# A two-block layer kernel on Trainium2: order of small matmuls among array tiles, order of DMA requests, place of a mean, and the form of eight units of products

## What is computed

```python
for i in range(2):                                   # first block
    u = rmsnorm(h) @ w_in[i]                         # 2048 -> 5632
    a_val, a_glu, a_z, q, k, v, b_z = split(u)
    ya = silu(layernorm(conv31(a_val * sigmoid(a_glu)))) * silu(a_z)
    yb = banded_attention(q, k, v, bias, sink) * silu(b_z)   # 16 heads of 64
    h = h + concat(ya, yb) @ w_out[i]
    h = h + rmsnorm(p[i] @ w_pe[i]) * sigmoid(h @ w_pg[i])
# second block: h @ w_in_2 -> RWKV-7 scan (16 heads of 64) and latent attention (8 heads),
# @ w_out_2, then a gated FFN of width 5632 with a convolution of width 3, and a last norm
```

## Time and profile before

| | us |
|---|---|
| median of 3 runs | 2280.56 |
| lowest, highest | 2279.8, 2282.35 |
| the profiled execution, whole | 2274.88 |
| its span in the trace | 2273.1 |
| PE busy in it | 2222.8 (98%) |
| PEld, DVE, ACT, POOL busy | 1968.8, 1690.8, 1068.1, 553.8 |
| DMA | 384.93 MB, 169 GB/s |
| request of a unit (1 MB) to landing, median | 4.8 |
| POOL's split of a unit (L241), mean | 4.6 |

### The profile page before, as it was taken

How to read it: one execution, slowest core, us unless ns; L and a number is a source line. 1 busy time by engine, 2 the same in 40 slices (tenths; PEclk the granted TensorE clock), 3 DMA queues, 4 the chain that set the end, 5 groups by cost and what they waited for, 6 DMA issues and landing times.

```text
span 2273.1 us, 39333 instructions
## 1 busy us (share of the span) xinstructions
PE 2222.8 (98%) x14865; PEld 1968.8 (87%) x14865; DVE 1690.8 (74%) x2863; ACT 1068.1 (47%) x1427; POOL 553.8 (24%) x226
## 2 busy tenths in 40 slices
PE   7999999999999999999999999999999999999997
PEld 6888998888888988899999887888888888888886
DVE  7688668885888488888878655778888885447887
ACT  5444464444444554556545522444444443334444
POOL 4776631017667520210002302110000000000012
PEclk9999999999999999999999999999999999999999
DMA  7445345555545355554444300455555555555564
GB/s 256 158 179 178 140 167 186 185 185 186 181 164 179 131 184 185 185 200 165 153 165 174 93 2 20 148 185 185 185 185 189 189 191 187 185 185 187 187 218 166
DMA packets 69034, 384.93 MB, mean 169 GB/s; under 512 B 15088, under 2 KB 22768, under 8 KB 23984
## 3 DMA queue, kind: packets, MB, share of 16 engines
q1 hardware_dynamic: 68912, 383.22, 47.6%
HBM read 380.02 MB, written 3.18 MB: 169 GB/s over the span
## 4 chain that ended last, share of the span: by engine, by line
PE 85%; DVE 5%; issue 3%; POOL 2%; ACT 2%; DMA 2%; SPq 0%; POOLq 0%; DVEq 0%; ACTq 0%
PE ps L259 40%; PE ps L260 21%; PE ps L247 4%; PE ps L249 4%; PE ps L248 4%; PE ps L262 3%; DMA raw<-weights_dram 1%; PE ps L870 1%; POOL low L241 1%; POOL ssq L1130 1%; DVE low L234 1%; PE ps L851 1%; PE ps L1939 1%; DVE ps L709 1%; PE ps L859 1%
## 5 line engine op out<-in xcount | busy, mean ns | idle before, releaser
L259 PE MATMUL ps<-opA,whi 128*128 128x512 f32 x2340 | 828.4, 394 | 1.5 <-POOL low L241 1.5
L229 ACT ACTIVATE whi<-raw 128x2048 fp32r<-128x2048 f32 x346 | 660.2, 1909 | 87.3 <-DMA raw<-weights_dram 85.6
L260 PE MATMUL ps<-opA,low 128*128 128x256 f32 x2496 | 672.6, 279 | 0.2 <-DVE opA L987 0.2
L234 DVE TENSOR_TENSOR low<-raw,whi 128x2048 fp32r<-128x2048 f32 x252 | 577.3, 2291 | 65.2 <-ACT whi L229 49.6
L241 POOL TENSOR_TENSOR low<-raw,whi 128x2048 fp32r<-128x2048 f32 x95 | 436.5, 4607 | 444.0 <-ACT whi L229 417.5
L259 PEld LDWEIGHTS ps<-opA,whi 128*128 128x128 f32 x2340 | 438.7, 187 | 102.1 <-issue 2.5
L260 PEld LDWEIGHTS ps<-opA,low 128*128 128x128 f32 x2496 | 468.1, 188 | 13.7 <-DVE opA L987 0.5
L259 PE MATMUL ps<-opB,whi 128*128 128x512 f32 x1260 | 453.6, 399 | 17.6 <-DVE opB L408 11.7
L260 PE MATMUL ps<-opB,low 128*128 128x256 f32 x1344 | 364.5, 281 | 0.0
L268 ACT ACTIVATE crossed<-ps 128x256 f32<-128x256 f32 x168 | 64.5, 384 | 516.1 <-PE ps L262 515.9
L259 PEld LDWEIGHTS ps<-opB,whi 128*128 128x128 f32 x1260 | 238.5, 189 | 76.4 <-DVE low L402 10.5
(11 more groups left out here) (396 smaller groups left out, 2981.3 us busy)
## 6 DMA issues: line engine op xcount, KB each, us to landing
raw<-weights_dram SPq DMA_DIRECT2D x350, 1024.0 KB, 4.8
bias_t<-table_dram SPq DMA_DIRECT2D x16, 384.0 KB, 6.1
hT<-xT_dram SPq DMA_DIRECT2D x4, 512.0 KB, 9.0
out_dram<-hT SPq DMA_DIRECT2D x4, 512.0 KB, 2.9
lora_g<-lora_dram SPq DMA_DIRECT2D x1, 1024.0 KB, 5.0
p_in<-pT_dram SPq DMA_DIRECT2D x2, 256.0 KB, 2.7
lora_wa<-lora_dram SPq DMA_DIRECT2D x1, 512.0 KB, 5.4
chunk_mats_dram<-compact SPq DMA_DIRECT2D x4, 128.0 KB, 3.2
```

Source lines behind the costliest of these rows:

```text
L229: act.activation(whi[:, v % RING, :], raw[:, v % RING, :], ACT.Copy).then_inc(hi_done.sem, 1)
L234: v_.tensor_tensor(wlo(v % RING, 0, width), raw[:, v % RING, 0:width], whi[:, v % RING, 0:width].bitcast(F32), ALU.subtract).then_inc(lo_d ...
L259: pe.matmul(*cross, start=start, stop=False)
L260: mm = pe.matmul(ps[:, b, 0:T], wlo(s, w0, w0 + P), op[:, k, 0:T], start=False, stop=False)
```

## The change

Six edits in one. (1) SP's order in the front: each `sp_unit` comes first; `p_in` is asked for at m = 1, `flip_eye` and the table at m = 2, `bias(0)` at m = 4, `bias(1)` at m = 6. (2) `even(0)` stands before ACT's split of unit 46, `even(2)` before `affine(6)`; `odd(1)` before `mixed(7)`, `odd(3)` before `product(6)`. (3) Units 36 to 43 are wide, and DVE adds their halves, after it has waited for ACT's `gate` of the unit before. (4) The mean's matmuls stand within unit 37, after three of its 16 steps. (5) `scores` of the attention and `lower_pe` have the heads as the inner loop. (6) So have the three groups of `phase_within`; the state steps take four tiles in turn.

```diff
@@ phase_front, SP
-                if l:
-                    sp.wait_ge(*ready(KB))
                 for m in range(46):
-                    if m == 2 and l == 0:
-                        sp.wait_ge(*table_sb(1))
-                        sp.dma_start(table[:, 0, :], tb[:, :]).then_inc(table_out.sem, 16)
-                        sp.wait_ge(*table_out(16))
-                    if m == (0 if l else 2):
+                    sp_unit(sp, u0, m)
+                    if m == 1:
+                        if l:
+                            sp.wait_ge(*ready(KB))
                         sp.dma_start(p_in[:, :, :], pT[l, :, :, :].rearrange("k p t -> p k t")).then_inc(fr["p_in"].sem, 16)
+                    if m == 2:
                         sp.dma_start(flip_eye[:, :], consts[3, :, :]).then_inc(fr["flip_in"].sem, 16)
+                        if l == 0:
+                            sp.wait_ge(*table_sb(1))
+                            sp.dma_start(table[:, 0, :], tb[:, :]).then_inc(table_out.sem, 16)
+                    if m == 4:
+                        if l == 0:
+                            sp.wait_ge(*table_out(16))
                         bias(0)
+                    if m == 6:
                         bias(1)
-                    sp_unit(sp, u0, m)
@@ phase_front, ACT
                 for m in range(46):
+                    if m == 44:
+                        even(0).then_inc(fr["even_read"].sem, 1)
                     if m >= 3 * ahead:
                         act_split(act, u0, m)
...
                     if m == 44:
-                        even(0).then_inc(fr["even_read"].sem, 1)
+                        even(2).then_inc(fr["even_read"].sem, 1)
                     if 41 <= m < 45:
                         affine(2 * (m - 41))
                         affine(2 * (m - 41) + 1)
                     if m == 44:
-                        even(2).then_inc(fr["even_read"].sem, 1)
                         even(4).then_inc(ev_done.sem, 1)
@@ phase_front, DVE
                     else:
                         v.wait_ge(mm_done.sem, u0 + m + 1)
+                        v.wait_ge(*fr["gate"](GATED.index(m - 1) + 1))
+                        src = ps[:, 6, T:2 * T]
+                        link(add_halves(v, (u0 + m) % 2, src))
...
                 gated(43)
+                odd(1)
                 mixed(PAIRS - 1)
                 conv_low(4)
                 conv_low(5)
-                odd(1)
+                odd(3)
                 product(6)
                 product(7)
-                odd(3)
@@ phase_front, PE
-                    pe_unit(pe, u0, m, 0, op, ready=ready if m == 0 else None, wide=m < 36)
+                    pe_unit(pe, u0, m, 0, op, ready=ready if m == 0 else None, wide=True, within=(3, mean) if m == 37 else None)
...
-                    if m == 36:
-                        pe.wait_ge(*fr["conv"](1))
-                        for c in range(CB):
-                            mm = pe.matmul(ps[:, 5, 0:T], ones[:, :], y_ln[:, c, :], start=c == 0, stop=c == CB - 1)
-                        mm.then_inc(fr["mean"].sem, 1)
@@ scores of phase_within (scores of phase_front and lower_pe swap their two loops likewise)
-                for h in range(2):
-                    r = slice(DH * h, DH * h + DH)
-                    pe.matmul(ps[:, 3 + h, 0:P], a_gate[r, pair, t], r_[r, pair, t], start=True, stop=True)
-                    pe.matmul(ps[:, 3 + h, P:2 * P], k_[r, pair, t], kk[r, pair, t], start=True, stop=True)
-                    mm = pe.matmul(ps[:, 3 + h, 2 * P:3 * P], k_[r, pair, t], r_[r, pair, t], start=True, stop=True)
+                for x, (w, y) in enumerate(((a_gate, r_), (k_, kk), (k_, r_))):
+                    for h in range(2):
+                        r = slice(DH * h, DH * h + DH)
+                        mm = pe.matmul(ps[:, 3 + h, x * P:x * P + P], w[r, pair, t], y[r, pair, t], start=True, stop=True)
@@ phase_within, state steps (the outputs, L1924 to L1926, are split into three loops over h likewise)
-                        for c in (2 * half, 2 * half + 1):
-                            s = slice(CH * c, CH * c + CH)
-                            for h in range(2):
...
+                        tiles = [(6 * half + c, slice(CH * (2 * half + c), CH * (2 * half + c) + CH), h) for h in range(2) for c in range(2)]
+                        for b, s, h in tiles:
+                            pe.matmul(ps[head[h], b, 0:DH], aq[s, y, h, 0:DH], chunk_ends[s, pair, sc, 0, head[h]], start=True, stop=True)
+                        for b, s, h in tiles:
+                            pe.matmul(ps[head[h], b, DH:P], chunk_ends[s, pair, sc, 0, head[h]], aq[s, y, h, DH:P], start=True, stop=False)
+                        for b, s, h in tiles:
+                            mm = pe.matmul(ps[head[h], b, DH:P], chunk_ends[s, pair, sc, 1, head[h]], tokV[s, y, head[h]], start=False, stop=True)
```

35 lines of the change are left out of this document (18 added, 17 removed).

## The result

| | before | after |
|---|---|---|
| median of 4 runs each, on one chip | 2280.18 | 2246.45 |
| lowest, highest | 2275.48, 2282.35 | 2242.93, 2248.56 |
| ratio, 95% interval | | 0.9851 [0.9839, 0.9863] |
| the profiled execution | 2274.88 | 2245.08 |

The change is faster by 33.7 us in the medians and by 29.8 us between the two profiled executions. The forecast was 22.0 us less, 2258.6, with a range down to 2252: the direction is right, and the gain is larger than the range allowed.

A forecast was written before the change was run, and what follows sets the result against it. PE, busy for 98% of the span, was taken as the bound. Requests 3.4, mean 1.6, wide units with `even` and `odd` 4.6 and `phase_within` 12.4 sum to 22.0 us: 2280.56 to 2258.6, range 2252 to 2271.

The forecast's parts named there:

- the term of the state steps: State steps of `phase_within`, tiles in turn at the chain's rate per instruction: 0.19 us an item, 3.1 us in all.
- Scores of `phase_within`: Both row tiles start together, so the score block ends 0.33 us earlier in 15 items: 5.0 us.
- A period of `phase_within` set by ACT's `aq`: Sign listed as showing the forecast wrong: ACT's `aq` copy, given 0.65 us of slack, would set the item's period.
- Outputs: Output products of `phase_within`, heads in turn: 0.27 us in each of 16 items, 4.3 us.
- The rival that column tiles can't be fed in turn: Outputs of `phase_within` need head 0's lead for their loads, so their 4.3 us goes: 2262.9; chance 0.10.
- Requests: Weight requests ahead of side transfers in both fronts: PE's two waits for POOL's `low` go, 3.4 us.
- Mean: Mean's matmuls inside unit 37 cover PE's waits for the last tap: about 0.8 us per layer, 1.6 us.
- Wide units, `even` and `odd`: Eight wide units per front, 1.2 us a layer, and earlier `even` and `odd` copies: together 2.3 per layer, 4.6 us.
- The stall that was put down as next: At unit 46 of each front, PE would start at 322.0 instead of 321.6, held by DVE's split.
- Attention scores and `lower_pe`: Heads in turn there gain nothing, the pairs already running together; upper bounds 2.1 and 0.8 us.
- The slower rival: Tile changes sharing a side in state steps and outputs of `phase_within` cost 0.2 us each: 2304.4; chance 0.03.

The follow-up runs named there:

- states_only: The kernel before with the new order of the state steps of `phase_within` and nothing else: 2265.56 us, against 2281.52 for the kernel before in the same set.
- states_old: The changed kernel with the state steps of `phase_within` alone put back, each tile's three matmuls one behind another: 2258.60 us.
- aq_first: The changed kernel with ACT copying `aq` as soon as its product is there, ahead of the token copies and `step_out`: 2245.79 us.
- outputs_old: The changed kernel with the output products of `phase_within` alone in the old order, three per head in a row: 2252.82 us.
- within_old: The changed kernel with all three orders of `phase_within` put back, the rest of the change kept: 2269.62 us.

## Why the prediction was right in direction and short in size

**The step that failed** is the term of the state steps, "At 29.7 ns they take 1.43, at 32.2 they take 1.55, which saves 0.25 or 0.13. Middle 0.19 x 16 = 3.1." It took the chain's 29.7 ns for the rate of PE's queue. It is the slot of a tile, 58 ns, divided by the chain's two tiles. With four tiles the rate is twice as high, and the two halves overlap as well: the block went from 1.68 to 0.76 us, 0.92 an item in place of 0.19. That is 14.7 us alone (16.0 measured in states_only) and 11.8 within the change (12.2 in states_old). The 32.2 was a misreading besides: it contains the 0.15 us from the block's last start to the next full-array product, and its own starts are 29 ns apart like the others. The row beside it did not tell the two readings apart: in the earlier trace rows the second tile starts 0.17 us after the first, and six instructions at 29.7 ns are 0.18. What would have told them is the distance of one tile's own instructions, 58 ns with a neighbour's in between, in states_old as in the kernel before. A rate read where two tiles work bounds what four can do from one side only, and I gave it as both ends.

Taken one after the other the parts fit the trace: states_old has the scores and outputs in turn and an item 0.60 us shorter than before, which is 0.33 + 0.27 as forecast, and the state steps then bring 0.74 more. 16 x 1.34 is 21.4, and 21.2 were measured.

The Trainium skill speaks on both sides here, in "TensorE: Matmul & The Clock Gate". Its section "Wait — 56ns, not 53.3ns?" has the distance of about 25 ns below which two starts never come; I weighed that rule, and here starts of different tiles lie 6 to 7 ns apart, so between tiles it does not hold. Its sections "The mechanism" and "Measured speedup vs the span model" give about 4 ns between starts on different tiles, which is near what the trace shows.

**Scores of `phase_within`** (forecast 5.0): the order works, both row tiles start together, and beside the old state steps the full 0.33 arrives (states_old). Beside the new ones it is 2.4 us in all. The prediction compared 0.33 of gain with 0.65 of slack at ACT's `aq`. That slack held only while the state steps took 1.68 us: `step_out` already began with the end of DVE's last read (1375.10 and 1375.12), and when the state steps shrank by 0.92, this read, and `aq` with it, came 0.44 us later behind G. So this miss follows from the first. "A period of `phase_within` set by ACT's `aq`" was on the list of signs that would be wrong, and it is what happened; aq_first shows it.

**Outputs** (forecast 4.3): 0.27 us an item, 4.3 us, right. The rival that column tiles can't be fed in turn is refuted: the two heads' matmuls start together, and outputs_old loses exactly this. The rule of the Trainium skill's section "The mechanism" ("TensorE: Matmul & The Clock Gate"), that loads overlap only across row groups, does not hold for these column tiles: in the change's trace both heads' loads for the next L1932 run at 1346.12 to 1346.27, inside the L1932 products that both heads have running from 1346.07 to 1346.40.

**Requests** (forecast 3.4): right for layer 1 (1.7 against 1.5). In layer 0 A is 2.1 to 2.3 us earlier where the clock did not fall on the way, against 1.9 forecast. Without the new order, with the rest of the change in place, there is an execution that loses 6.4.

**Mean** (1.6): 2.1. **Wide units, `even` and `odd`** (4.6): 3.4. `even` and `odd` came as forecast, 1.2 us a layer against 1.1; the wide units brought 0.5 against the 1.2 that 0.15 a unit had given. The stall that was put down as next, for DVE's split of unit 46, is there with 0.3 us a layer. **Attention scores and `lower_pe`** (0): 0.1. That the fronts' 9.7 meets the forecast's 9.6 so closely is luck in part: requests and mean came out 0.5 us over each, the wide units with `even` and `odd` 1.2 under.

**The slower rival** read a change of tile shape at 0.2 us rightly (in the change the last output starts at 1346.67 and the first state step at 1346.88), but it is refuted in taking that price over to a change of side: those happen each 6 to 7 ns in the state steps.

**Against the medians.** 9.6 of the 22.0 were outside `phase_within`, and within_old measures 11.9 there, with a scatter of some 2 us. Of the missing 11.7 us the larger part, 8.8 in the traces, is `phase_within`, and the rest, 2.9, is of the size of the scatter from execution to execution.

## What to carry to other kernels

Where small products use a part of the array, order them so that neighbours in the queue lie on different tiles: here the next tile did not start before the third of a run of six instructions on one tile. Two tiles in turn gave 0.66 of the 0.92 us that four gave, and eight only 0.05 more. A rate that is read from rows with n tiles at work belongs to a tile, so ask what it is per tile before it is used as the engine's. When a block on the bound engine shrinks by more than the slack of its helpers, compare the slack with the new period, not with the old: the copy that waits for another engine's last read belongs behind the copies that the bound engine waits for.

## What the runs showed of the hardware that was not expected

- Starts on different tiles lie 6 to 7 ns apart in full float32, in rounds over four or eight tiles. Behind 32 instructions of a block with eight tiles in turn, and behind 34 with four, most starts lay 16 to 17 ns apart; why stays open.
- A tile takes its next instruction each 0.058 us, for 64 columns and (in the chain) for 32 columns alike; between the first and the second of a block with 64 columns it is 0.107.
- Behind a run of six instructions on one tile, or of two times six on a pair, the next tile starts right behind the third: after 0.17 us (32 rows, 64 columns), 0.27 (column tiles, 128 columns) and 0.33 (row tiles, 128 columns). In the attention scores of the kernel before, with four instructions of 256 columns on a tile, it did not wait: the second instruction to start is 0.012 us behind the first, where those of one tile lie over 0.2 apart.
- The same waits on PE are followed by a lower granted clock in one execution and not in the next (0.83 in 1160 to 1170 us in one trace, 1.00 in another of the same kernel). Stretch C varies by 5 us in code that is the same, and its length goes with the number of these falls; behind a wait of 3.4 us at 53.5 us the mean granted clock of ten us was 0.66.
